# Expert stage of a two-layer diffusion trunk: one up half piece moved ahead of the down half pieces

## What is computed

```python
def expert_block(args):
    xi, e = args
    a = jnp.einsum('cd,df->cf', xi, w_gate[e])
    b = jnp.einsum('cd,df->cf', xi, w_up[e])
    return jnp.einsum('cf,fd->cd', jax.nn.silu(a) * b, w_down[e])
```

## Time and profile before

| what | value |
| --- | --- |
| runs, median (lowest to highest) | 2421.56 us (2415.51 to 2426.61) |
| profiled execution, its time | 2423.01 us |
| profiled execution, span of its instructions | 2421.1 us |
| PE busy | 2149.9 us, 89% of the span |
| DVE, ACT, POOL busy | 1225.2, 817.8, 253.5 us |
| chain that ended last | PE 71%, DVE 15%, ACT 6%, DMA 3% |
| expert stage, first product to last | about 887 to 1200 us and 2064 to 2377 us |

### The profile page before, as it was taken

How to read it: one execution, slowest core, us unless ns; L and a number is a source line. 1 busy time by engine, 2 the same in 40 slices (tenths; PEclk the granted TensorE clock), 3 DMA queues, 4 the chain that set the end, 5 groups by cost and what they waited for, 6 DMA issues and landing times.

```text
span 2421.1 us, 25630 instructions
## 1 busy us (share of the span) xinstructions
PE 2149.9 (89%) x10487; PEld 1600.9 (66%) x10487; DVE 1225.2 (51%) x1630; ACT 817.8 (34%) x1030; POOL 253.5 (10%) x222
## 2 busy tenths in 40 slices
PE   1899989999999969999749999999999995899992
PEld 0587565588885557777627855647888744777771
DVE  0286454223223368887555745532232244888883
ACT  1124532100000147777432254321000012677771
POOL 2133010200000110000021401001000000000002
PEclk9999989999999869999969999999999995999996
DMA  7226340311214379999551336011211313899993
GB/s 265 99 71 228 141 148 1 122 35 70 102 38 174 100 281 375 380 378 378 213 202 35 107 141 208 9 70 53 105 35 70 122 69 130 297 381 380 378 354 148
DMA packets 113911, 417.13 MB, mean 172 GB/s; under 512 B 7800, under 2 KB 9960, under 8 KB 89088
## 3 DMA queue, kind: packets, MB, share of 16 engines
q1 hardware_dynamic: 89088, 329.27, 37.0%
q0 software_dynamic: 19920, 68.31, 7.5%
q10 hardware_dynamic: 4784, 17.87, 1.8%
HBM read 378.89 MB, written 36.54 MB: 172 GB/s over the span
## 4 chain that ended last, share of the span: by engine, by line
PE 71%; DVE 15%; ACT 6%; DMA 3%; issue 3%; SPq 0%; ACTq 0%; PEldq 0%; POOL 0%; DVEq 0%; POOLq 0%
PE ps L652 61%; DVE expert_low L1856 7%; PE ps L770 3%; ACT expert_high L1389 3%; PE ps L782 2%; PE ps L663 2%; DVE x_low L1862 2%; DMA ring_lo<-in_w_mod_dram 1%; ACT branch L1422 1%; ACT x_high L1394 1%; DVE work L1881 1%; DVE hidden_low L1868 1%; DMA work<-y_dram,slots_u 1%; DVE work L1624 1%; PE ps L771 1%
## 5 line engine op out<-in xcount | busy, mean ns | idle before, releaser
L1856 DVE TENSOR_TENSOR expert_low<-ring_lo,expert_high 128x2048 fp32r<-128x2048 f32 x192 | 433.2, 2286 | 26.6 <-ACT expert_high L1389 26.6
L1389 ACT ACTIVATE expert_high<-ring_lo 128x2048 fp32r<-128x2048 f32 x192 | 367.3, 1915 | 162.9 <-PE ps L652 134.7
L652 PE MATMUL ps<-ring_lo,hT 128*128 128x512 f32 (+1 forms) x800 | 317.3, 554 | 12.5 <-ACT hT L1203 12.3
L652 PEld LDWEIGHTS ps<-ring_lo,hT 128*128 128x128 f32 x800 | 150.8, 192 | 161.3 <-issue 157.6
L652 PE MATMUL ps<-expert_high,x_high 128*128 128x512 f32 x512 | 208.0, 406 | 9.6 <-DVE expert_low L1856 9.6
L652 PE MATMUL ps<-branch,ring_lo 128*128 128x320 f32 x768 | 214.4, 432 | 0.0
L652 PE MATMUL ps<-expert_high,x_low 128*128 128x512 f32 x512 | 202.3, 395 | 0.0
L652 PE MATMUL ps<-expert_low,x_high 128*128 128x512 f32 x512 | 201.3, 393 | 0.0
L1338 ACT ACTIVATE work<-ps 128x640 f32<-128x640 f32 x48 | 33.8, 704 | 485.5 <-PE ps L652 485.4
L652 PE MATMUL ps<-h_hi,w_hi 128*128 128x320 f32 x768 | 186.2, 324 | 2.6 <-issue 2.6
L652 PEld LDWEIGHTS ps<-branch,ring_lo 128*128 128x128 f32 x768 | 143.5, 190 | 53.3
(11 more groups left out here) (270 smaller groups left out, 3142.1 us busy)
## 6 DMA issues: line engine op xcount, KB each, us to landing
ring_lo<-in_w_gate_dram SPq DMA_DIRECT2D x64, 1024.0 KB, 8.4
ring_lo<-in_w_up_dram SPq DMA_DIRECT2D x64, 1024.0 KB, 7.1
ring_lo<-in_w_down_dram SPq DMA_DIRECT2D x64, 1024.0 KB, 7.7
ring_lo<-in_w_in_dram SPq DMA_DIRECT2D x26, 2048.0 KB, 8.1
ring_lo<-in_w_mod_dram SPq DMA_DIRECT2D x24, 2048.0 KB, 13.5
y_dram<-branch ACTq DMA_DIRECT2D x32, 512.0 KB, 9.1
ring_lo<-in_w_out_dram SPq DMA_DIRECT2D x4, 2048.0 KB, 8.3
work<-mod_dram POOLq DMA_DIRECT2D x12, 512.0 KB, 9.3
```

The source lines that it names most:

```text
L652: return pe.matmul(out, lhsT, rhs, start=(k == 0), stop=(k == n - 1))
L1389: A(e_high[n % HIGH], e_raw[n % RAW], ACT.Copy).then_inc(ec_a.sem, 1)
L1856: TT(out=e_low[n % RAW], in0=e_raw[n % RAW], in1=e_high[n % HIGH].bitcast(F32), op=ALU.subtract).then_inc(el_v.sem, 1)
```

## The change

It moves the first up half piece of an expert from behind the down pieces of the expert before to a place ahead of them. The table of turns becomes:

```diff
         for e in range(NE + 1):
             if e < NE:
-                turns += [("gate", e, 0), ("gate", e, 1)]
+                turns += [("gate", e, 0), ("gate", e, 1), ("up", e, 0)]
             if e >= 1:
                 turns += [("down", e - 1, 0), ("down", e - 1, 1)]
             if e < NE:
-                turns += [("up", e, 0), ("up", e, 1)]
+                turns += [("up", e, 1)]
```

## The result

The changed kernel takes 2378.25 us (median of 4 runs, 2377.09 to 2381.76) where the kernel before takes 2420.41 us (4 runs, 2415.51 to 2426.61): a ratio of 0.9821, 95% interval 0.9801 to 0.984, some 42 us. The profiled execution took 2381.76 us with a span of 2379.9 us. A second measurement with more runs gave 2377.61 us (5 runs) against 2421.72 us (9 runs), 0.9818 [0.9803, 0.9833], some 44 us.

The account below looks back on a forecast made before the run. PE was busy almost everywhere, with DMA nearly full in expert stages. Removing hidden_low waits was worth 42 us; transfers at 18.7 us per expert left 15 us a layer, 30 us in both: 2423 - 30 = 2393, forecast 2392 us, range 2378 to 2413.

Parts of the forecast that it names:

- The wait and its price: PE's waits for hidden_low before down 0, 32 falling to 2; full price 42 us over both layers.
- I take 18.7 us: Transfer time assumed per expert, 0.75 us slower than PE's 17.95, leaving 30 us of the 42 us gain.
- The end at 425 GB/s: Fast case for the expert stages' transfers: 7.34 MB take 17.3 us per expert, so all 42 us are kept.
- the stretch at 318 GB/s: The 8 us around the end of down 1, where slower transfers were said to lose 2.0 us per expert.
- the free lateness: Some 5 us loads may slip before PE waits, 0.75 us used per expert: 6.5 experts at full gain.
- The cause of the wait: Gate 1 is too short a cover: inner values' way through ACT and DVE ends 1.2 us behind it.
- the margin of 2.4 us: PE reaches down 0 at 987.9, hidden_low being there since 985.42, so the wait is gone.
- Queues: SP, ACT and POOL loads change order, not number; store and fetch move about 8 us apart, no price by itself.
- The transfers have room: Rival: expert transfers take 17.3 us each, the full 42 us is gained, 2380 us; chance 0.20.
- The transfers pace it fully: Rival: 19.0 us of transfers per expert, gain 12 us at most, perhaps 8, 2413 us; chance 0.14.
- Store and fetch apart make it worse: Rival: each brings its own slow stretch, 21.0 us per expert, 2457 us; chance 0.05.
- The wait only moves: Rival: PE waits as long for the product of inner values instead of hidden_low, 2421 us; chance 0.03.

Follow-up runs that it names:

- the up piece alone: The change's order of pieces, but turn of rows, x_high and x_low left behind down 1, against the kernel before: 2452.72 us, ratio 1.0137.
- the second store: The changed kernel with each down product stored a second time from ACT's queue, 7.86 MB per expert: 2402.79 us, ratio 0.9925 to the kernel before.
- inner values ahead of the cast: The kernel before with only hidden_high and hidden_low one turn earlier on ACT and DVE: 2377.3 us, ratio 0.982.
- start and tail: The changed kernel with three splits ahead of the first x_low and the last expert's up 1 before the previous expert's downs: 2369.7 us, again 2370.65 us.
- the rows' turn alone: The kernel before, piece order kept, with turn of rows, x_high and x_low done ahead of down 0: 2384.53 us, ratio 0.9857.
- the store's issue moved: The kernel before with ACT's issue of the down product's store moved behind the next cast and x_high: 2406.62 us, ratio 0.9942.

## Why the prediction was right and wrong

**The wait and its price: right in size.** 32 waits became two, the two named, down 0 follows up 0 at once, and PE's floor was 17.86 us where 17.95 were worked out. The full price of 42 us is what was measured (2420.4 - 2378.3 = 42.1; 44.1 in the second measurement). Two small errors lie in it and about cancel: each expert gained 19.40 - 17.86 = 1.54 us and not 1.45, some 3 us over both layers (most of it because the first matmul behind a wait is followed after 0.31 us, 985.67 to 985.98, and not after 0.23), and the lower clock at the ends of the layers (last section) took about as much back. That the price held is in part luck: by the same reasoning the up piece alone would have gained it too, and it lost 32 us.

**The transfers: the step that failed.** "I take 18.7 us" for an expert's transfers was mis-sized; they need at most 17.35 us (the second store, 423 GB/s). The end at 425 GB/s, which stood in the text, was the right one. I was led off it twice. First by the DMA share: a share of 0.96 to 1.01 I took as perhaps full, but it was 0.96 to 1.01 at 370 to 386 GB/s before, 1.00 at 360 with the up piece alone, 1.01 at 402 to 414 after and 1.02 at 424 with the second store, so a share near 1 does not say how far the limit is. Second by the stretch at 318 GB/s, priced as a loss of 2.0 us per expert that partly stays. The rate in a stage paced by a loop is only what the loop asks for: with a gap of 0.58 us taken out of the loop it rose of itself, from 378 to 390 GB/s. Hence the free lateness and the 6.5 experts were worked out for nothing; experts stay at 17.86 us to the end. Why just that stretch ran at 318 GB/s stays open.

**The cause of the wait: wrong, and the measured time does not show it.** "ACT is in a cast until 983.19" and "DVE is in two splits until 984.82" were read correctly, but I did not ask why DVE was so late. It had stood still 2.78 us for x_high, which stood behind a cast, a store issue and the copy. "The only steps that move are x_high on ACT and x_low on DVE ... they cannot become the wait", at a cost of nothing: in this change that move holds the gain, since without it the kernel is 32 us slower than before, and without the up piece 36 us are won. That the margin of 2.4 us would be kept was true, even too cautious: hidden_low was done 3.6 us ahead of its use.

**Queues: harmless, as said.** In the first layer's stage (900 to 1170 us) loads land after 7.7 us in the median and 9.3 at most, against 7.5 and 10.4 before.

**The rivals.** *The transfers have room*: this came true, at 2380 forecast. *The transfers pace it fully*: no load paces an expert in the change; ACT waits for loads 1.4 us in all in the first layer's stage (900 to 1190 us). Whole experts move 402 to 414 GB/s, and 424 with the second store. The Trainium skill's share of 358 GB/s for one core (DMA: Bandwidth & Descriptors, section Bandwidth) is therefore not what binds here; the same section says that the share holds with both cores of an HBM domain streaming, and gives 425 GB/s as measured for a core alone, with which the trace agrees. *Store and fetch apart make it worse*: the rate rose instead, and with both together (inner values ahead of the cast) it is the same. *The wait only moves*: not in the change; but the run with the up piece alone shows that it does just that, to x_low, when the rows' turn stays where it was.

## What to carry to other kernels

When an engine waits a little in every turn of a loop, follow the releasers back, through in-order neighbours that wait for nothing themselves, until an instruction meets its own next turn: if the steps add up to the period, shorten any of them, on whatever engine, before you look for a longer cover. Price a step that moves by what it stood behind and in front of, not by its own length. Before a transfer limit enters a sum, do not read it from the busy share; add a transfer from a queue that is idle and see whether the period changes.

## What was not expected of the hardware

The busy share of the DMA engines was 1.00 at 360 GB/s (the up piece alone), 0.98 at 370 (before) and 1.02 at 424 (the second store): from the first to the last, the busy time per byte falls by 13%, so the share hardly tells them apart. Issuing one store on ACT took 0.34 us and a second right behind it 0.45 us, and on the loop each was paid in full. POOL's fetch took 1.06 us with DVE idle and 2.29 us beside three splits of DVE (start and tail); what in DVE's work slows it was not tried. At the ends of the layers, behind the same two waits of PE (0.85 and 1.6 us), the matmuls of the last downs ran at the full clock in the kernel before and not in the change. The columns behind the busy times are clock, DMA share and GB/s. The windows of the first 12 of them, before (second layer) and after (first layer):

```profile
2371.34:2374.10 2.76, 2.76 (x12) 2.29 (x13) 0.00 (x0) 0.00 (x0) 0.00 (x0) 1.00 0.00 0
```

```profile
1175.57:1179.99 4.42, 4.42 (x12) 3.53 (x13) 0.00 (x0) 0.00 (x0) 0.00 (x0) 0.61 0.00 0
```

A granted clock of 0.61 is a mean: most of the stretch at 1.2 GHz, the rest at 2.4 GHz. It cost 4.42 - 2.76 = 1.7 us, and in the second layer, where the matmuls slow down only from the third on, about as much. One difference ahead of it is that PE had stood still for 1.26 us in each expert before and was busy without a break after. That does not decide it. With the rows' turn alone, where hardly an expert waits, the clock stays up; with the store's issue moved, where PE still waits some 0.7 us in each expert, it falls (first layer both, first 12 and first 14 matmuls):

```profile
1174.88:1177.60 2.72, 2.72 (x12) 2.27 (x13) 0.00 (x0) 0.00 (x0) 0.00 (x0) 1.00 0.00 0
```

```profile
1184.90:1190.60 5.70, 5.70 (x14) 4.46 (x15) 0.00 (x0) 0.00 (x0) 0.00 (x0) 0.50 0.00 0
```

What does decide it stays open.
